# Two-layer block, mixture-of-experts part: scatter weights turned at an expert's head, outputs copied half by half, one transfer for the seventh tile, nested else on TensorE

## The reference

```python
logits = h @ w_router                       # 256 x 8
top_val, top_idx = lax.top_k(logits, 2)
gate = jax.nn.softmax(top_val, axis=-1)
# for each expert e, over the tokens that chose it:
y_e = (silu(x_e @ w_gate[e]) * (x_e @ w_up[e])) @ w_down[e]   # 1024 -> 3584 -> 1024
y[token] += gate * y_e
```

## Time and profile before

| what | value |
|---|---|
| median of 3 runs | 1768.75 us |
| lowest, highest | 1766.95, 1779.86 us |
| the profiled execution's own time | 1774.51 us |
| its span, first to last instruction | 1772.7 us |
| mean granted TensorE clock | 0.959 of full speed |
| busy in the span: TensorE, VectorE, ScalarE | 1594.6 (90%), 409.1 (23%), 226.2 (13%) us |
| read from HBM | 480.49 MB |

### The profile page before, as it was taken

How to read it: one execution, slowest core, us unless ns; L and a number is a source line. 1 busy time by engine, 2 the same in 40 slices (tenths; PEclk the granted TensorE clock), 3 DMA queues, 4 the chain that set the end, 5 groups by cost and what they waited for, 6 DMA issues and landing times.

```text
span 1772.7 us, 19682 instructions
## 1 busy us (share of the span) xinstructions
PE 1594.6 (90%) x8282; PEld 872.2 (49%) x8283; DVE 409.1 (23%) x867; ACT 226.2 (13%) x439; POOL 0.2 (0%) x4
## 2 busy tenths in 40 slices
PE   5999889999989998797597999999999998999975
PEld 5778658777658784432132333334444433333321
DVE  4265523323333633400101002002000110100103
ACT  1122210000011321110011011111011001111101
POOL 0000000000000000000000000000000000000000
PEclk9999899999989998799799999999999999999998
DMA  9955525665745440099999999897666599999995
GB/s 348 326 203 177 190 95 190 237 237 190 262 136 181 167 181 19 3 378 371 342 389 371 382 378 370 327 389 279 248 248 235 208 327 388 370 389 371 389 371 217
DMA packets 168108, 482.18 MB, mean 272 GB/s; under 512 B 10472, under 2 KB 20992, under 8 KB 167936
## 3 DMA queue, kind: packets, MB, share of 16 engines
q1 hardware_dynamic: 168064, 481.57, 74.3%
HBM read 480.49 MB, written 1.05 MB: 272 GB/s over the span
## 4 chain that ended last, share of the span: by engine, by line
PE 74%; SPq 8%; DVE 8%; DMA 6%; issue 3%; ACT 2%; DVEq 0%; ACTq 0%
PE bank L830 14%; PE bank L879 10%; PE bank L640 7%; SPq L527 6%; PE bank L841 6%; PE bank L777 6%; PE bank L826 6%; PE bank L791 4%; DMA ring<-in_w_exp_down 4%; DVE acc L1004 4%; PE bank L759 3%; PE bank L873 3%; PE bank L634 2%; PE bank L962 2%; SPq L533 1%
## 5 line engine op out<-in xcount | busy, mean ns | idle before, releaser
L830 PE MATMUL bank<-ring,hT 128*64 128x448 f32 x1792 | 353.8, 545 | 45.6 <-issue 19.3
L879 PE MATMUL bank<-ring,bt 128*32 128x256 f32 (+1 forms) x1680 | 239.9, 495 | 24.5 <-DMA ring<-in_w_exp_down 12.3
L830 PEld LDWEIGHTS bank<-ring,hT 128*64 128x64 f32 x1792 | 130.0, 137 | 265.9 <-issue 205.9
L1342 DVE TENSOR_TENSOR bt<-bt,bank 128x448 f32<-128x448 f32 (+1 forms) x52 | 32.4, 622 | 807.6 <-PE bank L830 555.0
L879 PEld LDWEIGHTS bank<-ring,bt 128*32 128x32 f32 (+1 forms) x1680 | 86.0, 125 | 160.5 <-issue 119.1
L777 PE MATMUL bank<-hT,ring 128*128 128x256 f32 x704 | 156.0, 383 | 1.2 <-DVE hT L1075 1.2
L640 PE MATMUL bank<-hT,ring 128*128 128x256 f32 x640 | 152.9, 396 | 2.3 <-ACT hT L1424 1.2
L777 PEld LDWEIGHTS bank<-hT,ring 128*128 128x128 f32 x704 | 134.6, 192 | 21.7 <-issue 1.9
L640 PEld LDWEIGHTS bank<-hT,ring 128*128 128x128 f32 x640 | 124.4, 198 | 23.4 <-DVE hT L1075 3.1
L1004 DVE SCALAR_TENSOR_TENSOR acc<-ring,cond,acc 128x512 f32<-128x512 f32 x160 | 120.3, 752 | 5.6
L841 PE MATMUL bank<-ring,hT 128*32 128x448 f32 x1024 | 102.9, 542 | 0.0
(11 more groups left out here) (204 smaller groups left out, 999.8 us busy)
## 6 DMA issues: line engine op xcount, KB each, us to landing
ring<-in_w_exp_gate SPq DMA_DIRECT2D x128, 896.0 KB, 10.4
ring<-in_w_exp_up SPq DMA_DIRECT2D x128, 896.0 KB, 15.1
ring<-in_w_exp_down SPq DMA_DIRECT2D x64, 1536.0 KB, 16.3
ring<-in_w_ada SPq DMA_DIRECT2D x24, 2048.0 KB, 10.4
ring<-in_w_in SPq DMA_DIRECT2D x10, 2048.0 KB, 11.1
ring<-in_w_exp_down SPq DMA_DIRECT2D x64, 256.0 KB, 16.8
ring<-in_w_ff_gate SPq DMA_DIRECT2D x5, 2048.0 KB, 18.6
ring<-in_w_ff_up SPq DMA_DIRECT2D x5, 2048.0 KB, 14.0
```

The costliest lines, as they stand in the source:

```text
L830: last = mm(o[64 * c2:64 * c2 + 64, 0:EH], xsT[:, k, t0:t0 + 64], w[:, k, c2 * EH:(c2 + 1) * EH], start=(k == 0), stop=(k == KC - 1))
L879: last = mm(bank[4 + 2 * u][m * c:m * c + m, 0:D // parts], hsT[:, u, at_:at_ + m], ed[:, t, c * (D // parts):(c + 1) * (D // parts)], sta ...
```

## The change

What it does, on each queue:

- SP: the seventh tile of down is one transfer of 128 rows, from a source view with the two blocks as its outer dimension; `full_d[2]` counts 16 a step instead of 32.
- TensorE: `scatter_matrix`, the turning of `selg`, is called at an expert's head and goes to bank 1. The scatter waits for ScalarE's copies and does the left half of the columns, then for VectorE's and does the right half, into banks 2, 3, 6 and 7. Before up's first matmul of each step it waits for `sgt_a`. The wait for cleared banks stands ahead of the first turn (or quarter). The loop's head is placed at the start of an instruction fetch block (`head_slot` 0); it waits for `xsT_v` before it reads the class, and the classes are nested in else branches, so that after a body the code goes to the loop's end.
- ScalarE: copies the turned weights at the head (`scatter_matrix`); at the end it copies the left half of all outputs.
- VectorE: makes the next scatter weights at the start of `expert_end`, not after the clearing; no longer copies the turned weights; copies the right half of all outputs; adds the sums by column half.

```diff
                 room(J, TAIL - D, TAIL, d_used, 3 * J)
-                for i in range(2):
-                    r0 = j0 + i * EH + 3 * P
-                    sp.dma_start(ed[64 * i:64 * i + 64, 6, :], w_exp_down[0, e, r0:r0 + 64, :]).then_inc(full_d[2], 16)
+                last = w_exp_down[0, e, j0:j0 + EW, :].rearrange("(i r) n -> i r n", i=2)[:, 3 * P:EH, :]
+                sp.dma_start(ed[:, 6, :], last).then_inc(full_d[2], 16)
...
+                    if i == 0 and a == 1 and k == 0:
+                        pe.wait_ge(sgt_a, r + 1)
...
-                        pe.wait_ge(full_d[t // 3], (32 if t == 6 else 16) * J + (32 if t == 6 else 16))
+                        pe.wait_ge(full_d[t // 3], 16 * J + 16)
...
-            def scatter(r, n):
-
-                tiles = range(2 if n > 2 else 1)
+            def scatter_matrix(r, n):
+
                 pe.wait_ge(selg_v, r + 1)
-                for q in tiles:
+                for q in range(2 if n > 2 else 1):
                     for b in range(2):
-                        last = nc.tensor.transpose(bank[0][:, q * T + b * P:q * T + (b + 1) * P],
+                        last = nc.tensor.transpose(bank[1][:, q * T + b * P:q * T + (b + 1) * P],
                                                    selg[:, b, q * P:(q + 1) * P], ident)
                 last.then_inc(sgt_p, 1)
-                pe.wait_ge(ys_v, r + 1)
-                pe.wait_ge(ys_a, r + 1)
-                for b in range(2):
-                    for hf in range(2):
+
+            def scatter(r, n):
+
+                tiles = range(2 if n > 2 else 1)
+                for hf in range(2):
+                    pe.wait_ge((ys_a, ys_v)[hf], r + 1)
+                    for b in range(2):
                         for q in tiles:
-                            last = mm(bank[4 + 2 * b + hf][:, :], selgT[:, q, b * P:(b + 1) * P],
+                            last = mm(bank[(2, 6)[hf] + b][:, :], selgT[:, q, b * P:(b + 1) * P],
...
+            def expert(r, n):
+
+                scatter_matrix(r, n)
+                with pe.Fori(0, ES) as s:
+                    step(r, r * ES + s, n)
+                scatter(r, n)
+
+            PE = (mybir.EngineType.PE,)
+            with nc.Fori(0, NE, engines=PE, head_slot={PE[0]: 0}) as r:
+                pe.wait_ge(xsT_v, r + 1)
                 which = class_of(pe, r)
-                pe.wait_ge(xsT_v, r + 1)
-                for n in range(1, 5):
-                    with pe.If(which == n):
-                        with pe.Fori(0, ES) as s:
-                            step(r, r * ES + s, n)
-                        scatter(r, n)
+                with pe.If(which == 1):
+                    expert(r, 1)
+                with pe.Else():
+                    with pe.If(which == 2):
+                        expert(r, 2)
+                    with pe.Else():
...
@@ VectorE
                 window(r + 1)
-                tiles = 2 if n > 2 else 1
-                ve.wait_ge(sgt_p, r + 1)
-                last = nc.vector.tensor_copy(selgT[:, 0:tiles, :].rearrange("p q n -> p (q n)"), bank[0][:, 0:tiles * T])
-                if n > 1:
-                    ve.wait_ge(d_used, 3 * ES * r + 3 * ES)
+                scatter_weights(r + 1)
+                ve.wait_ge(d_used, 3 * ES * r + 3 * ES)
+                if n < 3:
+                    last = nc.vector.tensor_copy(ys[0:64, 0, CW:D], bank[4][64:P, :])
+                else:
+                    last = nc.vector.tensor_copy(ys[:, 0, CW:D], bank[5][:, :])
                 if n in (2, 3):
                     s0, q = (64, 0) if n == 2 else (0, 1)
-                    for c in range(4):
+                    for c in (2, 3):
...
                 ve.wait_ge(yacc_v, 4 * r + 5)
                 clear_banks()
-                scatter_weights(r + 1)
@@ ScalarE
+            def scatter_matrix(r, n):
+
+                tiles = 2 if n > 2 else 1
+                ae.wait_ge(sgt_p, r + 1)
+                act(selgT[:, 0:tiles, :].rearrange("p q n -> p (q n)"), bank[1][:, 0:tiles * T], ACT.Copy).then_inc(sgt_a, 1)
+
             def expert_end(r, n):
 
                 ae.wait_ge(d_used, 3 * ES * r + 3 * ES)
-                for hf in range(2):
-                    if UNITS[n][0][0] == "half":
-                        ins = act(ys[0:64, 0, hf * CW:(hf + 1) * CW], bank[4][64 * hf:64 * hf + 64, :], ACT.Copy)
-                    else:
-                        ins = act(ys[:, 0, hf * CW:(hf + 1) * CW], bank[4 + hf][:, :], ACT.Copy)
+                if n < 3:
+                    ins = act(ys[0:64, 0, 0:CW], bank[4][0:64, :], ACT.Copy)
+                else:
+                    ins = act(ys[:, 0, 0:CW], bank[4][:, :], ACT.Copy)
+                if n in (2, 3):
+                    s0, q = (64, 0) if n == 2 else (0, 1)
+                    for c in (0, 1):
+                        ins = act(ys[s0:s0 + 32, q, c * T:(c + 1) * T], bank[6][32 * c:32 * c + 32, 0:T], ACT.Copy)
...
```

More of the change, by code:

```diff
@@ L816, in _, with hidden @@
                 last.then_inc(gat_p, 1)
-            def hidden(J, n, i, a, unit, c=0):
+            def hidden(r, J, n, i, a, unit, c=0):
                 kind, t0 = unit
@@ L891, in step @@
                 if n == 1:
[L892 to L893 removed]
+                    hidden(r, J, n, 0, 0, A)
+                    hidden(r, J, n, 0, 1, A)
+                    pe.wait_ge(yzero_v, r + 1)
                     turn_hidden(J, n, 0, "half", bank[3])
[L895 removed]
                     down(J, n, 0, ALL, (0,))
                 elif n == 2:
[L898 to L899 removed]
+                    hidden(r, J, n, 0, 0, A)
+                    hidden(r, J, n, 0, 1, A)
+                    pe.wait_ge(yzero_v, r + 1)
                     quarter(B[1], range(0, 6))
@@ L966, in _ @@
             pe.wait_ge(route_v, 1)
-            with pe.Fori(0, NE) as r:
-                which = class_of(pe, r)
-                pe.wait_ge(xsT_v, r + 1)
-                for n in range(1, 5):
-                    with pe.If(which == n):
-                        with pe.Fori(0, ES) as s:
-                            step(r, r * ES + s, n)
-                        scatter(r, n)
+            def expert(r, n):
[6 more added lines that the diff above has]
+                pe.wait_ge(xsT_v, r + 1)
+                which = class_of(pe, r)
+                with pe.If(which == 1):
[4 more added lines that the diff above has]
+                    with pe.Else():
+                        with pe.If(which == 3):
+                            expert(r, 3)
+                        with pe.Else():
+                            expert(r, 4)
         @block.vector
@@ L1358, in expert_end @@
                 elif n == 4:
-                    for hf in range(2):
-                        last = nc.vector.tensor_copy(ys[:, 1, hf * CW:(hf + 1) * CW], bank[6 + hf][:, :])
+                    last = nc.vector.tensor_copy(ys[:, 1, CW:D], bank[7][:, :])
                 last.then_inc(ys_v, 1)
@@ L1375, in _ @@
                 ve.wait_ge(yacc_v, 4 * r + 1)
-                for b in range(2):
-                    for hf in range(2):
-                        ve.wait_ge(sct_p, 4 * r + 2 * b + hf + 1)
+                for hf in range(2):
+                    for b in range(2):
+                        ve.wait_ge(sct_p, 4 * r + 2 * hf + b + 1)
                         y_ = yacc[:, b, hf * CW:(hf + 1) * CW]
-                        tt(y_, y_, bank[4 + 2 * b + hf][:, :], ALU.add).then_inc(yacc_v, 1)
+                        tt(y_, y_, bank[(2, 6)[hf] + b][:, :], ALU.add).then_inc(yacc_v, 1)
                 ve.wait_ge(yacc_v, 4 * r + 5)
                 clear_banks()
-                scatter_weights(r + 1)
             ve.wait_ge(yacc_v, 4 * NE + 1)
@@ L1550, in step @@
                     turned_hidden(J, n, 3, 1, 1, bank[3])
+            def scatter_matrix(r, n):
+                tiles = 2 if n > 2 else 1
+                ae.wait_ge(sgt_p, r + 1)
+                act(selgT[:, 0:tiles, :].rearrange("p q n -> p (q n)"), bank[1][:, 0:tiles * T], ACT.Copy).then_inc(sgt_a, 1)
             def expert_end(r, n):
                 ae.wait_ge(d_used, 3 * ES * r + 3 * ES)
-                for hf in range(2):
-                    if UNITS[n][0][0] == "half":
-                        ins = act(ys[0:64, 0, hf * CW:(hf + 1) * CW], bank[4][64 * hf:64 * hf + 64, :], ACT.Copy)
-                    else:
-                        ins = act(ys[:, 0, hf * CW:(hf + 1) * CW], bank[4 + hf][:, :], ACT.Copy)
+                if n < 3:
[6 more added lines that the diff above has]
+                        ins = act(ys[s0:s0 + 32, q, c * T:(c + 1) * T], bank[6][32 * c:32 * c + 32, 0:T], ACT.Copy)
+                elif n == 4:
+                    ins = act(ys[:, 1, 0:CW], bank[6][:, :], ACT.Copy)
                 ins.then_inc(ys_a, 1)
```

38 lines of the change are left out of this document (19 added, 19 removed).

## The result

The changed kernel takes 2061.05 us (2055.11 to 2062.17, 4 runs) where the kernel before, on the same chip, took 1774.3 (1766.95 to 1781.89, 4 runs): a ratio of 1.161, with an interval of 1.154 to 1.167. The profiled execution has a span of 2059.5 us. The forecast was 1999 in a range of 1890 to 2200: the sign and the mechanism came out (16% slower for 13%), the size was 62 us short.

The account below looks back on a forecast made before the run. It took TensorE to bound some stretches and the weight stream others. From 1774.5 us profiled, +231 for later loads and -1.2 at the end gave 2004.3; less 5.8 for profiled over median, 1999 us, range 1890 to 2200.

Parts of the forecast that it names:

- Two engines: Seventh down tile: the merged transfer runs on 2 engines, so a load takes 38.8 us (36.1 to 46.4); chance 0.80.
- The tile at 13 us: Seventh down tile: its transfer adds 13 us to the 25.8 us of a load's other bytes.
- the lone 10.3: Seventh down tile, lower end: 262 KB on each of two engines at 25.4 GB/s take 10.3 us.
- A: Rival, seventh tile: cut over 16 engines at 407 GB/s, 37 us faster, 1732 us; chance 0.17.
- B: Rival, seventh tile: cut over 16 engines but pace still halved, 7.5 us faster, 1761 us; chance 0.03.
- C: Rival, seventh tile: two engines, every packet at double time, 46.4 us a load, 2197 us; chance inside the 0.80.
- D: Rival, instruction stalls: they move to each class's first call, 6.4 us at expert 4; no chance of its own.
- Start and head: Expert 0's head: TensorE waits for scatter weights and turns them before the first gate matmul, +2.7 us.
- Ends: Experts' ends: scatter 1.6 us after the last matmul instead of 2.69, together -3 us if TensorE-bound; final end -1.2.
- The stall: After expert 0: one jump instead of three cuts the 19.28 us stall to some 6 and saves 6 us of stream.
- my -7.5 for the rest: All edits but the tile: +2.7 (start), -6 (dry stream), -3 (ends), -1.2 (end), 7.5 us faster.

Follow-up runs that it names:

- the lone transfer: Kernel before plus three separately awaited loads after its last output; the two-block 512 KB transfer took 12.0 us, 128 contiguous rows 2.9.
- the contiguous pair: Kernel after and kernel before, each with tile seven as 128 rows contiguous in memory (time only): 1743.46 us (0.981) and 1740.91 us (0.978).
- the kernel with the halves turned apart: Kernel before with the second half's first 64 rows in tile seven, contiguous, and TensorE turning each half by itself: 1795.61 us, ratio 1.009.
- the kernel after with the pair put back: Kernel after with the seventh tile as two 64-row transfers again, all other edits kept: 1781.89 us, ratio 1.002.

## Why the prediction was right, and where its size was off

The forecast stands on two engines carrying the seventh tile while the whole load waits for them, and the runs bear it out. One term was too small, and the rest of the sum held. One reading in it was wrong without effect: the down loads hold 4% of the chain of the earlier trace rows, and the 6% are SP's L527.

**Two engines.** Right, and shown three ways: the packets fell by 960 as forecast, 2, 4 and 16 blocks gave 2, 4 and 16 engines, and the lone transfer has a share of 0.13. The rule of the Trainium skill (DMA: Bandwidth & Descriptors, Why a DMA increments its semaphore by 16 and not by 1) gives these three counts from the slowest dimensions, and the traces agree. GB/s near 285 was forecast and 268 came; the wait for the seventh tile in experts 2 and 3 is there. The stretch with two engines at work was to be 10 us and more a step and is mostly 4 to 9.

**The tile at 13 us.** This is the term that was mis-sized: 15.3 measured, so 41.1 us a load for 38.8. I had added 2.7 us to the lone 10.3, for packets that slow each other, and kept it small because the other 14 engines would run out of work in part of the time. They do, and that idle time (9 us) with the tile's own 1.3 is the lone price, as forecast. But in the rest of the time all packets are slower (261 GB/s at a share of 0.96), and that costs 4.9 us for the 2.7. The rest of the sum held with it: 15 loads x 2.3 = 35 us, and expert 4 starts at 1378.4 for 1346.5 (+32); it gives nothing back, expert 5 starts at 1581.3 for 1549.5 (+32); 26 x 2.3 = 60, and the last landing is at 2037.3 for 1980.3 (+57). The other 5 us of the 62 are no part of the kernel: I had taken 5.8 off because the profiled execution of the kernel before lay that far over its median, and the one of the kernel after lies 0.9 over. The chain of the kernel after there:

```profile
1374.71 3.70 PE bank L965 x8
1378.41 0.44 PE bank L954 x4
...
1581.28 0.43 PE bank L954 x2
...
2009.72 27.50 DMA ring<-in_w_exp_down
```

**The rivals.** A's mechanism (16 engines at 407) is real for one contiguous transfer and gives 1743 where I had 1732. But 16 engines are not enough for it, nor is writing all 128 partitions: 16 blocks do both and gave 1779.5, and B (16 engines, pace still halved) is the better name for that, if not for its 1761. C's price, double time for every packet, is excluded, but its cause is there by half: 15.3 lies midway between 10.3 and 20.6. D came: stalls of 4.3 and 1.3 us stand after the first expert of class 2 and of class 3, for the 6.4 at expert 4 that I had said.

**Start and head.** In the contiguous pair the first gate matmul comes 751.47 - 746.69 = 4.8 us after ScalarE's last piece with the change and 746.86 - 745.04 = 1.8 without: +3.0 for +2.7. The start of the kernel after, in its chain:

```profile
745.59 0.79 ACT ring L1513
...
749.90 0.52 DVE arena L1333 x2
...
750.47 0.69 PE bank L954 x2
751.15 13.52 PE bank L831 x64
```

Gate now stands behind the scatter weights and their turning, as said.

**Ends.** The contiguous kernel after, at expert 2's end:

```profile
1070.87 1.77 PE bank L879 x32
...
1074.07 3.70 PE bank L964 x8
1077.78 4.32 issue
1082.10 0.43 PE bank L953 x2
```

The scatter starts 1074.07 - 1072.64 = 1.4 us after the last down matmul (forecast 1.6, before 2.69) and takes 3.70 where it took 5.40 both before and with the contiguous tile alone; that part is loose, since the kernel with the halves turned apart has its 5.40 at expert 3 instead, without the edit. The start does what it was costed at. The 4.32 us behind it take it back.

**The stall.** A third of 19.3 was forecast, a fifth came (4.0). In the contiguous pair expert 0's scatter is 842.82 with the edits and 837.27 without (+5.6), expert 1's 950.94 and 953.15 (-2.2): the late start cost 5.6 us there for the 2.7, and the short stall gave back 7.8 for the 6. Then expert 2's -2.6 becomes +1.1 at expert 3 through the new stall, and the shorter ends bring expert 4 to -0.1. From there on the two kernels run level, to the last scatter (1721.99 and 1722.01), and the end after it gives 0.5 us for the 1.2. So my -7.5 for the rest failed at two terms: the start was too cheap, and D's stalls I had "inside the range" and not in the sum. In the kernel after, the stall behind expert 0 is gone altogether (the turning follows the scatter at once), covered as said by the wait for loads.

## What to carry to other kernels

Before two transfers are merged into one, look at the outer count of both access patterns. Here the bytes were shared by 2, 4 and 16 engines where the source had 2, 4 and 16 blocks and the destination 128 rows, and one transfer in eleven that ran on two engines made a load of 29 us one of 41. Merge only what is contiguous, or split so that 16 divides the outer count, and check it afterwards by the count of small packets; even then look at GB/s for dips. Where a stream is made faster, take from the windows which stretch has slack on the other engine before that engine is given the work that makes it possible.

## What the runs showed of the hardware that was not expected

- A transfer on two engines costs in two ways. In SP's queue its 15.3 us are 9 us of other engines without work, 1.3 of its own bytes and 5 of slower packets on busy engines (261 GB/s at a share of 0.96); issued by GpSimd it costs 5.6, and no engine idles.
- 16 blocks of 8 rows run on 16 engines into all 128 partitions and still dip to 236 GB/s; one block of 128 rows keeps 407.
- How far one kernel's runs spread does not follow from its dips alone. With the contiguous tile three kernels spread by 3 to 6 us (4 to 6 runs each), but the one that also turns by halves by 25 (12 runs); the kernel after with the pair put back spread by 23 (12 runs). The cause is open.
- The nested else moves TensorE's stalls: of 19.3 us after the first expert 4.0 stay, and 4.3 and 1.3 come after the first expert of each other class; with four separate ifs the 19.3 are back and the other two are gone.
